# The gates' bias stored beside the gates and summed by the merge's selection product, and the exponential table fetched at the end of the front

## What is computed

```python
def _front(x, c, w_ada, b_ada, g_norm, w_in):
    mod = jnp.dot(jax.nn.silu(c), w_ada) + b_ada
    shift, scale, gate = jnp.split(mod, 3, axis=-1)
    h = _rms(x) * g_norm * (1 + scale[:, None, :]) + shift[:, None, :]
    cols = jnp.einsum('btd,dn->btn', h, w_in)
    return _split(cols), gate

def _prompt_attention(q, k, v):                 # per block of 128 queries
    s = jnp.einsum('bqhd,bkhd->bhqk', qi, k).astype(jnp.float32) * SCALE
    s = jnp.where(kpos[None, :] <= qpos[:, None], s, -jnp.inf)
    p = jax.nn.softmax(s, axis=-1).astype(v.dtype)
    return jnp.einsum('bhqk,bkhd->bqhd', p, v)

def _merge(x, gate, o_a, o_b, g_a, g_b, w_pa, w_pb, w_out):
    m = jax.nn.sigmoid(g_a) * (o_a @ w_pa) + jax.nn.sigmoid(g_b) * (o_b @ w_pb)
    return x + gate[:, None, :] * (m @ w_out)
```

## Time and profile before

| | before |
|---|---|
| median of 3 runs | 1507.72 us (1507.63 to 1507.77) |
| the profiled execution's own time | 1509.55 us |
| its span | 1507.9 us |
| mean granted TensorE clock | 0.993 |
| TensorE (PE) busy | 1469.3 us, 97% |
| VectorE (DVE) busy | 860.4 us, 57% |
| ScalarE (ACT) busy | 555.1 us, 37% |
| GpSimd (POOL) busy | 369.9 us, 25% |

### The profile page before, as it was taken

The page is one execution under the profiler, slowest core; times in us unless marked ns, Lnnn a source line. Parts: engine busy times, 40 slices in busy tenths (PEclk is TensorE's granted clock), DMA queues, the critical chain, the costliest instruction groups (busy, mean ns, idle before and its releaser), DMA issues.

```text
span 1507.9 us, 36390 instructions
## 1 busy us (share of the span) xinstructions
PE 1469.3 (97%) x14538; PEld 1079.9 (72%) x14538; DVE 860.4 (57%) x1708; ACT 555.1 (37%) x1355; POOL 369.9 (25%) x483
## 2 busy tenths in 40 slices
PE   6999999998999999999999999999999999999998
PEld 3555567766888888787777777777777777777753
DVE  3153555656877777656576776867676522013533
ACT  3056544451222222243555546353545332210000
POOL 0000041230111111115131313222121045446452
PEclk9999999999999999999999999999999999999999
DMA  9813688843466566411112122121211216243311
GB/s 323 313 41 107 168 239 266 253 109 109 110 156 150 151 152 155 128 47 32 37 50 49 42 57 55 32 52 33 52 39 43 67 44 204 74 154 84 119 40 51
DMA packets 191541, 165.42 MB, mean 110 GB/s; under 512 B 38554, under 2 KB 169626, under 8 KB 190348
## 3 DMA queue, kind: packets, MB, share of 16 engines
q1 hardware_dynamic: 182092, 127.52, 30.4%
q0 software_dynamic: 8352, 32.52, 7.1%
q10 hardware_dynamic: 928, 3.05, 0.6%
HBM read 136.97 MB, written 26.08 MB: 108 GB/s over the span
## 4 chain that ended last, share of the span: by engine, by line
PE 84%; DVE 6%; issue 3%; DVEq 2%; ACT 2%; POOL 1%; DMA 1%; POOLq 1%; SPq 0%; ACTq 0%
PE me_bank L3224 13%; PE rw_bank L1867 10%; PE sa_psOs L1218 8%; PE sa_psS L1173 7%; PE pr_psZ L741 4%; PE me_bank L3262 3%; PE fr_bankL L307 3%; PE pr_psS L729 2%; PE rw_bank L1903 2%; PE fr_bankL L247 2%; PE sa_psT L1183 2%; DVE rw_gram L2726 2%; PE rw_bank L1879 2%; PE pr_psT L752 1%; PE pr_psO L762 1%
## 5 line engine op out<-in xcount | busy, mean ns | idle before, releaser
L1867 PE MATMUL rw_bank<-hT,big 128*128 128x288 f32 x336 | 94.2, 420 | 0.0
L1279 ACT COPY kpe<-sa_psS 128x512 f32<-128x512 f32 x64 | 34.4, 589 | 137.9 <-PE sa_psS L1173 137.9
L1017 POOL DMA_DIRECT2D big<-in_cache_kv x68 | 37.6, 553 | 156.0 <-issue 156.0
L741 PE MATMUL pr_psZ<-hT,qlT 128*128 128x288 f32 x256 | 74.9, 413 | 0.6 <-DVE pr_zraw L845 0.6
L1867 PEld LDWEIGHTS rw_bank<-hT,big 128*128 128x128 f32 x336 | 59.9, 190 | 15.3 <-issue 1.2
L3300 ACT COPY big<-me_bank 128x288 f32<-128x288 f32 x42 | 16.7, 398 | 144.8 <-PE me_bank L3224 144.8
L1017 POOL DMA_DIRECT2D pages<-in_cache_kv x68 | 37.5, 552 | 117.5 <-issue 117.5
L741 PEld LDWEIGHTS pr_psZ<-hT,qlT 128*128 128x128 f32 x256 | 47.5, 192 | 21.7 <-issue 9.8
L1218 PE MATMUL sa_psOs<-big,sa_ST 128*128 128x257 f32 x256 | 60.3, 386 | 0.0
L1218 PE MATMUL sa_psOs<-pages,sa_ST 128*128 128x257 f32 x256 | 60.3, 385 | 0.0
L1369 DVE TENSOR_TENSOR sa_ST<-sa_psT,kinvp 128x512 f32<-128x512 f32 x64 | 42.9, 679 | 28.2 <-PE sa_psT L1183 28.0
(11 more groups left out here) (652 smaller groups left out, 3723.6 us busy)
## 6 DMA issues: line engine op xcount, KB each, us to landing
big<-in_w_in SPq DMA_DIRECT2D x44, 512.0 KB, 4.1
big<-in_cache_kv POOLq DMA_DIRECT2D x68, 128.0 KB, 3.7
pages<-in_cache_kv POOLq DMA_DIRECT2D x68, 128.0 KB, 3.1
fr_wada<-in_w_ada SPq DMA_DIRECT2D x8, 1024.0 KB, 11.9
big<-in_cache_kv SPq DMA_DIRECT2D x60, 128.0 KB, 3.0
pages<-in_cache_kv SPq DMA_DIRECT2D x60, 128.0 KB, 3.1
qk_scratch<-oaT SPq DMA_DIRECT2D x32, 192.0 KB, 2.6
fr_wada<-in_w_ada SPq DMA_DIRECT2D x2, 2048.0 KB, 11.1
```

Of the source, the lines that this page charges most:

```text
L741: last = nc.tensor.matmul(psZ[h][:, 0:HT], M.wz[hp % 2][:, k, :], M.hT[:, k, h * HT:(h + 1) * HT], start=(k == 0), stop=(k == KT - 1))
L1017: e.dma_start(M.pages[s % 2][q * QP:(q + 1) * QP, g, :, 0:KL], src).then_inc(landed, 16)
L1279: nc.scalar.copy(S.rearrange("q (c p j) -> q p c j", c=2 * GP, p=GP)[:, :, cs, :], got[:, :, cs, :]).then_inc(copied, 1)
L1867: last = mm(into, held, moving, start=(k == 0 and n in (1, 2, 7)), stop=(k == K4 - 1), skip_group_check=True)
```

## The change

The bias is no longer loaded to the core (L149), nor added on VectorE (L620). SyncE stores rows 0 to 8 and 18 to 127 of `gate` to scratch, and writes the bias from its place in memory to the scratch rows 9 to 17 by a transfer of its own. The matrix `sel4` gets a second 1 for each token, at row 9 + (its conditioning row), so the same product that sums the four quarters adds the bias too. The semaphore `front_done` is gone. Its three waiters now wait for what lay behind it: ScalarE for `k_done`, GpSimd for `k_done` and `gate_sb`, SyncE for `gate_sb` (it has waited for `k_done` already). The count of the semaphore on the early transfers is raised by two transfers. ScalarE gets one more instruction behind the copies of `gate`, an exponential of the one-column tile `eps`, whose result nothing reads.

```diff
--- before.py
+++ after.py
@@ -67,7 +67,7 @@
         crow, esil = small[0:R, 0:D], small[0:R, D:2 * D]
         vrow, vcol, sum9 = sb("vrow", [3 * KT, P]), sb("vcol", [P, 3 * KT]), sb("sum9", [P, R])
         wada = [sb(f"wada{i}", [P, KT, 2, CW]) for i in range(2)]
-        mp, gate_b = sb("mp", [P, 512]), sb("gate_b", [R, D])
+        mp = sb("mp", [P, 512])
         mG, mS = sb("mG", [P, KT, R]), sb("mS", [P, KT, R])
         own = M.oaT[:, :, :].rearrange("p k t -> p (k t)")
         x, headsT = own.rearrange("p (b d) -> p b d", d=D), own[0:QK, 0:8 * 512].rearrange("p (n h t) -> p n h t", n=8, t=P)
@@ -95,7 +95,7 @@
         L = [ps(f"bankL{i}") for i in range(NB)]
         RB, B7 = [ps("bankR0"), ps("bankR1")], ps("bankM")
         bankQ, bankK, bankV, bankH = L[1:4], [L[4], RB[1]], [L[0], B7], RB[0]
-        c_in, fixed_in, tab_in, gate_b_in, up_in = sem("c_in"), sem("fixed_in"), sem("tab_in"), sem("gate_b_in"), sem("up_in")
+        c_in, fixed_in, tab_in, up_in = sem("c_in"), sem("fixed_in"), sem("tab_in"), sem("up_in")
         x_in, ada_in, lat_in = [sem(f"x_in{t}") for t in range(NB)], [sem("ada_in0"), sem("ada_in1")], [sem(f"lat_in{c}") for c in range(NC)]
         set_, c_sig, c_silu, c_tr, c_sb, x_sq, x_rt, x_n, x_tr, x_dve, x_act = (
             sem(n) for n in ("set", "c_sig", "c_silu", "c_tr", "c_sb", "x_sq", "x_rt", "x_n", "x_tr", "x_dve", "x_act"))
@@ -108,8 +108,8 @@
         spilled, v_spilled = [sem(f"spilled{n}") for n in range(8)], [sem("v_spilled0"), sem("v_spilled1")]
         w_v = I["w_in"].rearrange("(k p) n -> p k n", p=P)
         ada_v = I["w_ada"].rearrange("(k p) n -> p k n", p=P)
-        block, front_done, last_stored = M.block, sem("done"), sem("last_stored")
-        M.set_, M.cnew_done, M.front_done, M.front_stored, M.kn_sb, M.qc_sb, M.gate_sb, M.gate_mm = set_, cnew_done, front_done, stored, kn_sb, qc_sb, gate_sb, gate_mm
+        block, last_stored = M.block, sem("last_stored")
+        M.set_, M.cnew_done, M.k_done, M.front_stored, M.kn_sb, M.qc_sb, M.gate_sb, M.gate_mm = set_, cnew_done, k_done, stored, kn_sb, qc_sb, gate_sb, gate_mm
         rows = lambda t: SB if t == PB else P
 
         @block.sync
@@ -146,7 +146,6 @@
             sp.dma_start(wuq[:, :, :], I["w_uq"].rearrange("(k p) h d -> p k (h d)", p=P)).then_inc(up_in, 16)
             sp.dma_start(wuk[:, :, :], I["w_uk"].rearrange("(k p) h d -> p k (h d)", p=P)).then_inc(up_in, 16)
             sp.dma_start(wuv[:, :, :], I["w_uv"].rearrange("(k p) h d -> p k (h d)", p=P)).then_inc(up_in, 16)
-            sp.dma_start(gate_b[:, :], bc(I["b_ada"][2 * D:3 * D], R, 0)).then_inc(gate_b_in, 16)
             for n in range(2):
                 sp.wait_ge(part, n + 3)
                 sp.dma_start(wada[n][:, :, :, :].rearrange("p k a n -> p k (a n)"), ada_v[:, :, 2 * D + n * 512:2 * D + (n + 1) * 512]).then_inc(ada_in[n], 16)
@@ -486,6 +485,7 @@
             for n in range(2):
                 act.wait_ge(gate_mm, n + 1)
                 nc.scalar.copy(M.gate[:, n * 512:(n + 1) * 512], bankQ[n][:, :]).then_inc(gate_sb, 1)
+            nc.scalar.activation(eps[:, :], eps[:, :], ACT.Exp)
 
         @block.vector
         def _(dve):
@@ -615,9 +615,6 @@
             latents((4,), 2)
             for t in range(NB):
                 norms(t)
-            dve.wait_ge(gate_b_in, 16)
-            dve.wait_ge(gate_sb, 2)
-            v.tensor_tensor(M.gate[0:R, :], M.gate[0:R, :], gate_b[:, :], ALU.add).then_inc(front_done, 1)
 
 
 def prompt(nc, I, M):
@@ -636,7 +633,7 @@
         M.spare = pb[:, :, :].rearrange("p a t -> p (a t)")
         psS, psT, psO, psB = [ps(f"psS{i}") for i in range(3)], ps("psT"), ps("psO"), ps("psB")
         psZ = [ps("psZ0"), ps("psZ1")]
-        NG = BD * PAGES // P
+        NG, ROWS = BD * PAGES // P, 1 + BD
         listed = I["page_table"].rearrange("b n -> (b n)")
         page_of = ctx.enter_context(nc.sbuf_tensor("pr_page_of", [P, NG], I32))
         staged = M.pages[1][:, :, :, :].rearrange("p g c n -> p (g c n)")
@@ -670,8 +667,10 @@
             load(0)
             load(1)
             M.last_store(sp)
-            sp.wait_ge(M.front_done, 1)
-            sp.dma_start(M.gate_dram, M.gate[:, :]).then_inc(M.early_in, 16)
+            sp.wait_ge(M.gate_sb, 2)
+            for rows in (slice(0, ROWS), slice(2 * ROWS, P)):
+                sp.dma_start(M.gate_dram[rows, :], M.gate[rows, :]).then_inc(M.early_in, 16)
+            sp.dma_start(M.gate_dram[ROWS:2 * ROWS, :], bc(I["b_ada"][2 * D:3 * D], ROWS, 0)).then_inc(M.early_in, 16)
             for hp in range(2, NP):
                 sp.wait_ge(z_mm, 2 * (hp - 1))
                 sp.dma_start(M.wz[hp % 2][:, :, :], w_v[:, :, C_ZA + hp * P:C_ZA + (hp + 1) * P]).then_inc(M.wz_in[hp % 2], 16)
@@ -680,7 +679,8 @@
 
         @block.gpsimd
         def _(pool):
-            pool.wait_ge(M.front_done, 1)
+            pool.wait_ge(M.k_done, NB)
+            pool.wait_ge(M.gate_sb, 2)
             pool.wait_ge(M.front_stored, 80)
             for a in range(NG):
                 pool.dma_start(page_of[:, a:a + 1], listed[a * P:(a + 1) * P].rearrange("(p o) -> p o", o=1)).then_inc(pages_listed, 16)
@@ -901,7 +901,7 @@
                 act.wait_ge(z_mm, e + 1)
                 nc.scalar.activation(M.zraw[:, e // 2, e % 2 * HT:(e % 2 + 1) * HT], psZ[e % 2][:, 0:HT], ACT.Tanh, scale=0.5).then_inc(z_tanh, 1)
 
-            act.wait_ge(M.front_done, 1)
+            act.wait_ge(M.k_done, NB)
             act.wait_ge(M.cnew_done, 1)
             act.wait_ge(M.front_stored, 80)
             exponentials(0)
@@ -1453,7 +1453,7 @@
 HT = USED // 2
 
 
-EARLY_IN = 16 * (1 + 2 + 17 + 2)
+EARLY_IN = 16 * (3 + 2 + 17 + 2)
 
 
 def _load_vectors(sp, I, M):
@@ -3426,7 +3426,8 @@
     tok = np.arange(2 * P)
     owner = np.where(tok < P, 0, np.where(tok - P < SB, 1 + (tok - P) // TD, -1))
     row = i % 32
-    c["sel4"] = (owner[None, :] == row[:, None]).astype(np.float32)
+    bias_of = np.where((i > BD) & (i < 2 * (1 + BD)), i - (1 + BD), -2)
+    c["sel4"] = ((owner[None, :] == row[:, None]) | (owner[None, :] == bias_of[:, None])).astype(np.float32)
     c["sum9"] = (row[:, None] == np.arange(1 + BD)[None, :]).astype(np.float32)
     pos = np.concatenate([np.arange(SEQ), PAGES * PS + np.arange(P) % TD]).astype(np.float32)
     inv = np.float32(10000.0) ** (-np.arange(HALF, dtype=np.float32) / np.float32(HALF))
```

## The result

The change makes the kernel slower: 1516.94 us, the median of 8 runs (1513.15 to 1523.73), against 1507.68 for 8 runs of before (1506.06 to 1511.68). The ratio is 1.0066, with a 95% interval of 1.0052 to 1.0080. The profiled execution took 1521.05 us and its span is 1519.4 us, 11.5 more than the 1507.9 of before. It is one of the longer of the eight: the medians lie 9.3 us apart, and its mean granted clock is 0.987 where the others have 0.988 to 0.994.

A forecast was written before the change was run, and what follows sets the result against it. TensorE, holding 84% of the chain, was taken as the bound, waiting at the end of the front. Stall 2.06 plus clock 1.68 gave 3.74 us, taken from the median 1507.72: 1504.0 us, range 1502.0 to 1506.7.

The forecast's parts named there:

- The stall and the table: End of the front: without the bias add and with an early table load, gate piece 16 starts 2.06 us earlier.
- The clock: From gate piece 16 to the value products: the low clock near 189 goes, gaining 1.68 us, bounds 0 and 3.4.
- The transfers: SyncE's three transfers instead of one, ahead of pair 2's gate weights: 0.7 to 1.1 us in its queue, path effect zero.
- GpSimd: GpSimd starts at about 183.3 instead of 184.46, its page loads 1.1 us earlier: effect on the time zero.
- The slower rival: Pair 6: value load lands later as GpSimd's page loads overlap otherwise, TensorE waits, clock may fall: 1509.7 us, chance 0.07.

The follow-up runs named there:

- poolearly: Kernel before with GpSimd's earlier start alone (waits for `k_done` and `gate_sb` instead of `front_done`): 1506.84 us against 1508.33, ratio 0.9993.
- split: Kernel before with the three stores of the change, the bias rows not selected by `sel4`: median 1508.14 us, ratio 1.0012.
- late: Kernel before with pair 2's gate weights issued behind GpSimd's two gathers, nothing else changed: 1515.41 us, ratio 1.0051.
- table: Kernel before with the dummy exponential alone, its end signalling the second copy of the gates: 1505.28 us against 1506.40, ratio 0.9989.
- onestore: Kernel after with one gate store of 128 rows and no bias transfer (output lacks the gates' bias): 1502.88 us, ratio 0.9984 to before.
- bias: Kernel after without the dummy exponential: 1517.13 us (4 runs), ratio 1.0073 to before.
- first_b: Kernel after with pair 2's gate weights issued ahead of the three gate stores, one extra profiled execution: 1508.03 us.
- first_c: Kernel after with pair 2's gate weights issued ahead of the three gate stores, a second extra profiled execution: 1504.44 us.

## Why the prediction was wrong

Predicted were 1504.0 us and a gain of 3.7 us; measured were 1516.94 us and a ratio of 1.0066.

*The stall and the table:* right. The masking came 1.13 us earlier against the front (183.49 - 184.31 - 0.31), and gate piece 16 came 188.53 - 186.72 + 0.31 = 2.12 us earlier, where 2.06 was predicted. Together with the clock that is 3.8 us, against 3.74 predicted.

*The clock:* the size of the term was right. From gate piece 16 to the value products the kernel after takes 190.56 - 186.72 = 3.84 us, where the prediction has 3.85 and the kernel before took 5.53. Its reason is not shown. The late exponential and its stall stay in poolearly, split and late. The profiles of poolearly and split have no low clock there (193.60 - 189.76 and 192.99 - 189.15, both 3.84 us, behind waits of 0.76 and 0.56 us, and of 0.53 and 0.56), and that of late has it (194.48 - 188.96 = 5.52 us, behind 1.07 and 0.56). So the drop may stay away with the stall in place, and that it was absent in the profile of the change may be luck.

*The transfers:* this is the step that failed, in the words "even the slowest landing of rows 7, 10.6 us, leaves 12 us. ... The path gets nothing and loses nothing." The landing was 24.3 us. I had taken the bound from value loads, none of which was issued into the start of the gathers. The cover was misread as well. I took the matmuls at 210.14 for the first use of the weights, but piece 32 stood at 206.36 before. After the change TensorE would have come 3.5 us sooner still, at 202.86, which is 15.0 us behind the issue at 187.82. That covers a landing of 10.6 us and not one of 24.3: the 9.3 us between them are the wait (9.18 in the row). The step counted the two more issues in SyncE's queue (the weights went out at 187.82 instead of 186.27, 1.5 us later), and not how long the stores themselves occupy the transfer engines (59.8% of them at a time instead of 104.2%).

*GpSimd:* the second half of the same fault. "Zero" and "1.1 us earlier" looked at who waits for GpSimd, and not at whose transfers its own would meet. The gathers came 2.3 us earlier (187.10, not 189.38): GpSimd started 0.8 us earlier, and waited 1.49 us for the page table instead of 2.95. Before, SyncE issued the gate store 0.1 us behind GpSimd's load of the table (185.87 and 185.76); after, 1.3 us behind it (186.22 and 184.94). In late and in table the two are again within 0.3 us of each other, and the wait is 2.8 and 3.7 us; in split, onestore, poolearly and bias the store comes 0.4 to 1.7 us behind, and it is 1.5 to 1.9. No run changes this alone, but it fits that the one store had also held the gathers back. The weights moved back by 1.5 us and the gathers forward by 2.3: together 3.8 us, more than the lead of 3.1 us that the weights had.

*The slower rival* had part of the mechanism, transfers of GpSimd against a load that TensorE needs, with the low clock behind the wait. It had the wrong place (pair 6 instead of pair 2) and so a chance of 0.07. At pair 6 the trace after has no wait for the value load. It priced the low clock behind a wait at 1.7 us; behind one of 9.2 us it was 5.8.

## What to carry to other kernels

In this kernel SyncE's load and GpSimd's gathers, neither of which waits for the other, met on the transfer engines. So when a change moves one of them forward or the other back, check which large transfer now starts ahead of which small-packet load, and not only who waits for whom. A bound on a landing holds only for loads issued into the same traffic. Where a load of small packets is needed soon, issue it ahead of stores that can wait, and far enough ahead of a gather of large rows that its packets are through before the gather's begin. Here 0.4 us between the two issues was enough behind one store, and 0.2 us behind three was not. A clock drop behind a stall in one profile is no proof that filling the stall removes it: look for the same stall in the profiles of other runs.

## What the hardware showed beyond that

A load of 0.5 MB in 0.5 KB packets took 4.3 to 5.6 us when it was ahead of the gathers, and 18 to 24 us when it was caught by them.

The same place in the program may be at low clock in one execution and at full clock in another. Two executions of the same kernel (first_b and first_c), the same window:

```profile
343.00:350.00 7.00, 6.12 (x53) 5.39 (x55) 2.27 (x2) 1.17 (x2) 0.00 (x0) 0.51 0.81 206
```

```profile
343.00:350.00 7.00, 6.12 (x81) 4.69 (x80) 1.79 (x1) 1.87 (x4) 0.00 (x0) 1.00 0.77 196
```

One has it at 0.51 for 7 us and the other at 1.00, with the same 6.12 us of busy time, 53 matmuls against 81; they took 1508.03 and 1504.44 us. Ahead of the stretch the matmuls of L1194 start at 341.91 and 341.44 us, behind it those of L1201 at 351.76 and 348.46. The distance grows from 0.47 to 3.30 us, so this stretch accounts for 2.8 of the 3.6 us between the two. The mean clock also goes with the time of an execution, though the groups overlap: of 30 of the kernel before on one chip, those with a mean of 0.996 to 0.998 took 1504.9 to 1506.8 us, and those with 0.993 or 0.994 took 1506.1 to 1510.3; of 22 on another chip it was 1505.4 to 1509.0 and 1509.0 to 1511.5. So the 1.68 us that the prediction took for the clock at 189 is not a sure gain of filling the stall, as the prediction itself said of its bound of 0, but the price of a drop that an execution may or may not have.
